# A RWKV-7 block solve: one transposed diagonal copied instead, two result copies regrouped on ScalarE, one value copy moved ahead

## The reference, cut to what matters

```python
def rwkv7_scan(r, w, kk, kka, k, v, s0):
    def step(S, inp):
        r_t, w_t, kk_t, kka_t, k_t, v_t = inp
        sa = jnp.einsum('bzhvk,bzhk->bzhv', S, -kk_t)
        S = S * w_t[..., None, :] + sa[..., None] * kka_t[..., None, :] + v_t[..., None] * k_t[..., None, :]
        return S, jnp.einsum('bzhvk,bzhk->bzhv', S, r_t)
```

## Time and profile before

| | |
|---|---|
| time, median of 3 runs | 3142.31 us (3141.88 to 3144.67) |
| the profiled execution: time, span | 3141.88 us, 3140.1 us |
| busy: PE / DVE / ACT / POOL | 96% / 58% / 34% / 13% |
| chain that ended last: PE / DVE / ACT | 83% / 8% / 3% |
| layer 0's chunks (843 to 1040 us): length, PE / DVE / POOL busy | 197.0, 169.0 / 137.6 / 64.9 us |
| layer 1's chunks (2383 to 2585 us): length, PE / DVE / POOL busy | 202.0, 172.8 / 134.3 / 65.0 us |

### The profile page before, as it was taken

The page is one execution under the profiler, slowest core; times in us unless marked ns, Lnnn a source line. Parts: engine busy times, 40 slices in busy tenths (PEclk is TensorE's granted clock), DMA queues, the critical chain, the costliest instruction groups (busy, mean ns, idle before and its releaser), DMA issues.

```text
span 3140.1 us, 62825 instructions
## 1 busy us (share of the span) xinstructions
PE 3005.7 (96%) x26760; PEld 2700.9 (86%) x26760; DVE 1823.1 (58%) x2658; ACT 1073.1 (34%) x1609; POOL 412.0 (13%) x465
## 2 busy tenths in 40 slices
PE   6999999999988899999999999999998889999998
PEld 5999978996777799998799998799776777999986
DVE  3767555656766767765657675633666666222235
ACT  3111244235443531113531113532454435211134
POOL 1000101002233310001100001110033323000100
PEclk9999999999899999999999999999998989999999
DMA  5344334310000333333433333422010003121134
GB/s 225 133 160 160 120 128 155 124 41 27 30 4 13 123 132 148 131 144 134 148 147 133 148 147 127 148 101 84 15 50 7 13 33 126 67 80 67 64 124 167
DMA packets 62635, 324.09 MB, mean 103 GB/s; under 512 B 8752, under 2 KB 12400, under 8 KB 42992
## 3 DMA queue, kind: packets, MB, share of 16 engines
q1 hardware_dynamic: 62448, 321.39, 27.9%
HBM read 318.05 MB, written 3.31 MB: 102 GB/s over the span
## 4 chain that ended last, share of the span: by engine, by line
PE 83%; DVE 8%; DMA 3%; issue 3%; ACT 3%; POOL 0%; SPq 0%; DVEq 0%; ACTq 0%; POOLq 0%
PE PS L2474 47%; PE PS L2557 16%; PE PS L2485 3%; DMA wo<-in_wo 3%; PE PS L696 2%; PE PS L1470 2%; DVE wo_lo L2876 1%; ACT wo_hi L2671 1%; PE PS L720 1%; PE PS L1449 1%; PE PS L643 1%; PE PS L1462 1%; DMA wm<-in_wm 1%; PE PS L708 1%; PE PS L1393 1%
## 5 line engine op out<-in xcount | busy, mean ns | idle before, releaser
L2474 PE MATMUL PS<-h_hi,wi_hi 128*128 128x384 f32 (+1 forms) x3360 | 799.0, 310 | 11.1 <-issue 10.9
L2474 PE MATMUL PS<-h_lo,wi_hi 128*128 128x384 f32 (+1 forms) x3360 | 797.3, 309 | 0.0
L2474 PE MATMUL PS<-h_hi,wi_lo 128*128 128x384 f32 (+1 forms) x3360 | 797.3, 309 | 0.0
L2474 PEld LDWEIGHTS PS<-h_hi,wi_hi 128*128 128x128 f32 x3360 | 526.3, 188 | 14.2 <-issue 13.4
L2474 PEld LDWEIGHTS PS<-h_hi,wi_lo 128*128 128x128 f32 x3360 | 526.2, 188 | 0.7
L2474 PEld LDWEIGHTS PS<-h_lo,wi_hi 128*128 128x128 f32 x3360 | 525.9, 188 | 0.7
L2557 PE MATMUL PS<-wo_hi,a_hi 128*128 128x512 f32 x968 | 392.9, 406 | 21.3 <-DVE wo_lo L2876 13.8
L2876 DVE TENSOR_TENSOR wo_lo<-wo,wo_hi 128x1024 fp32r<-128x1024 f32 x208 | 256.2, 1232 | 253.8 <-ACT wo_hi L2671 253.1
L2664 ACT ACTIVATE sg<-PS 128x640 f32<-128x640 f32 x88 | 62.2, 706 | 937.4 <-PE PS L2474 937.4
L2557 PE MATMUL PS<-wo_hi,a_lo 128*128 128x512 f32 x968 | 378.4, 391 | 0.0
L2557 PE MATMUL PS<-wo_lo,a_hi 128*128 128x512 f32 x968 | 378.1, 391 | 0.0
(11 more groups left out here) (324 smaller groups left out, 3804.2 us busy)
## 6 DMA issues: line engine op xcount, KB each, us to landing
wi<-in_wi SPq DMA_DIRECT2D x88, 1024.0 KB, 4.9
wo<-in_wo SPq DMA_DIRECT2D x176, 512.0 KB, 3.5
wm<-in_wm SPq DMA_DIRECT2D x36, 2048.0 KB, 7.4
wi<-in_win SPq DMA_DIRECT2D x24, 1024.0 KB, 5.2
wo<-in_wout SPq DMA_DIRECT2D x32, 512.0 KB, 3.5
wq<-in_wq SPq DMA_DIRECT2D x2, 1024.0 KB, 4.8
out_y_sample<-x SPq DMA_DIRECT2D x4, 512.0 KB, 5.5
lvl<-in_lvl SPq DMA_DIRECT2D x2, 896.0 KB, 6.0
```

Source lines behind the costliest of these rows:

```text
L2474: mm = pe.matmul(PSF[0:cols, at:at + GW[g]], st, h[g][:, k, :], start=(k == 0 and q == 0), stop=(k == KD - 1 and q == 2))
```

## The change

Three edits in `solve`, and the semaphores that they need. (1) On DVE the four transposes L2139 become four `tensor_copy` instructions from `XTc[1]`, the same size, SBUF to SBUF. (2) The copy of `Zs[1]` goes from DVE (L2157) to ACT, right behind `Zs[0]`; in the last chunk DVE's `beside(5)` therefore follows `beside(4)` directly, and ACT's `Zs[1]` stands ahead of its own `beside(5)`. (3) In chunks 0 to 3 ACT's `values_out(c, 0)` goes ahead of `diagonal(c)`. The two semaphores `t10` and `t11` become one, on which the two directions' events alternate.

```diff
-        stage("t10", 30)
-        stage("t11", 30)
+        series("level_lx_out", 30, "t10", "t11")
...
+                if not last:
+                    values_out(c, 0)
                 diagonal(c)
                 if last:
                     beside(3)
                 else:
-                    values_out(c, 0)
                     values_out(c, 1)
...
-                until(a_, l, "t1_mm0", 5 * c + 5)
-                a_.activation(Zs[0][64:P, :, :].rearrange("p h t -> p (h t)"), PS[64:P, 4 ^ f, :], ACT.Copy)\
-                    .then_inc(S["t10"].sem, 1)
+                for d in range(2):
+                    until(a_, l, f"t1_mm{d}", 5 * c + 5)
+                    b = slice(64, P) if d == 0 else slice(0, 64)
+                    a_.activation(Zs[d][b, :, :].rearrange("p h t -> p (h t)"), PS[b, (4 + 2 * d) ^ f, :], ACT.Copy)\
+                        .then_inc(S[f"t1{d}"].sem, 1)
...
                 for q in range(4):
                     at = slice(q * QUAD, (q + 1) * QUAD)
-                    m = v_.transpose(XT[1][at, :, at], Xc[1][at, :, :])
+                    m = v_.tensor_copy(XT[1][at, :, at], XTc[1][at, :, :])
                 m.then_inc(S["xt1"].sem, 1)
...
                 if last:
                     beside(3)
                     beside(4)
+                    beside(5)
                 else:
                     prep(c + 1, 2)
                     prep(c + 1, 3)
-                mm_("t1_mm1", 5 * c + 5)
-                mm_("gh_mm1", c)
-                v_.tensor_copy(Zs[1][0:64, :, :].rearrange("p h t -> p (h t)"), PS[0:64, 6 ^ flip(c), :])\
-                    .then_inc(S["t11"].sem, 1)
-                if last:
-                    beside(5)
-                else:
                     prep(c + 1, 4)
```

## The result

| | before | after |
|---|---|---|
| time, median (range) | 3142.36 us, 4 runs (3141.88 to 3144.67) | 3163.36 us, 4 runs (3161.49 to 3168.25) |
| profiled execution: time, span | 3141.88, 3140.1 us | 3157.67, 3155.9 us |
| ratio, 95% interval | | 1.0063 (1.0049 to 1.0077) |

The change made the kernel slower by 21 us; I had forecast 3153.1 us, and 3159 as the upper end. The direction was right and the size about half. The profiled execution took 3157.67 us, 15.8 more than the profiled one of before and 5.7 less than after's median, so the trace shows a quicker execution than the median one.

What follows compares the result with a forecast made beforehand. In chunks 0 to 3 DVE from L2010 to L2024 was taken to set the end. Terms 11.0 + 1.3 + 0.1 - 1.2 = +11.2 us gave 3153.1 us, range 3144 to 3159 (forecast's own 3150 to 3158).

Steps and rivals of the forecast that it cites:

- Which unit is held, and by what: Chunks 0 to 3: DVE's SBUF-to-SBUF copies wait while a POOL mask runs; free, 0.23 us each; transposes never over 309 ns.
- One copy through at each gap: Between POOL's masks one DVE copy gets in per gap; in chunk 2, L2010 starts 1.84 us later.
- the six chunks that I counted: All four of layer 0, chunks 1 and 2 of layer 1, where L2010 starts 0.13 behind POOL's end: +1.84 us each.
- the term of the held copies: L2010 delayed behind POOL's masks: 6 x 1.84 = +11.0 us, and +1.3 us in layer 1's chunk 0.
- through early: Rival, 0.20: copies finish before the third mask, which is stretched; 3145.2 us, or 3146.8 with two copies per gap.
- not held: Rival, 0.15: copies with stepped destination avoid the shared way, under 0.3 us beside masks; only -1.2 stays, 3140.7 us.
- One sign of a wrong forecast: L1417 no longer waiting for DVE would mean ACT's order or Zs[1] has become the limit.
- ACT's edits at 0, and −1.2 in the last chunks: Value copy first and Zs[1] on ACT hide in chunks 0 to 3; last chunks gain 0.6 us per layer.
- the clock was a rival with 0.04: More PE idling drops a few stretches to the lower clock, some 1.5 us each, up to 3159; chance beyond 3159: 0.04.

Runs made afterwards that it cites:

- the run with five matmuls: Changed kernel plus five 256-column PE matmuls, output overwritten, in front of L1455 in chunks 0 to 3: ratio 1.0033 to the kernel before.
- both stalls: Changed kernel with transposes back, in chunks 0 to 3 repeated by eight more transposes: ratio 1.0065; by four more: 1.0016, to the kernel before.
- the first four kernels: Against the kernel before: transposes back in the changed kernel 0.9982, copies alone 1.0056, eight more transposes without copies 1.0065, changed kernel plus ten matmuls 1.0062.

## Why the prediction was half right

**Which unit is held, and by what: right.** Copies of 0.2 us take up to 1.34 beside the masks, the transposes never over 0.31, and without masks none takes over 0.224 (forecast 0.23 free). The Trainium skill ("SBUF — State Buffer", section "Who interferes with whom") says of a VectorE copy in a two-port mode and a GpSimd instruction that whichever issues first has the shared port pair for the whole instruction and the other fully blocks; the trace agrees: two copies of chunk 2 last 1.21 us, as long as the masks' steps, and the masks stay at 1.25 to 1.29 us each.

**One copy through at each gap: right.** DVE's copies and POOL's last two masks in after's chunk 2, one by one:

```profile
952.63 1.02 DVE L2141 COPY XT<-XTc 32x128 f32<-32x128 f32 x1
953.66 1.21 DVE L2141 COPY XT<-XTc 32x128 f32<-32x128 f32 x1
954.89 1.21 DVE L2141 COPY XT<-XTc 32x128 f32<-32x128 f32 x1
956.11 0.22 DVE L2141 COPY XT<-XTc 32x128 f32<-32x128 f32 x1
...
953.53 1.27 POOL L2267 TENSOR_TENSOR LK<-LK,mask 128x512 f32<-128x512 f32 x1
954.75 1.27 POOL L2267 TENSOR_TENSOR LK<-LK,mask 128x512 f32<-128x512 f32 x1
```

The copies end at 953.65, 954.87, 956.10 and 956.33, the masks at 953.57, 954.80 and 956.02. The tiny copy falls to 0.17, L1455's delay grows by 2.40 (forecast 2.4), and L2012 starts 1.82 us later than L2010 had (4.44 to 6.26 behind L1677; forecast 1.84). In the six chunks that I counted it is 1.73 to 1.87, 10.9 together (forecast 11.0), and in layer 1's chunk 0 1.69 (forecast 1.3). So the term of the held copies, as DVE shows it, had the right size.

**The rivals "through early" and "not held": out.** The first asked for stretched masks and copies done before the third one, the second for copies under 0.3 beside a mask. Neither is there. One sign of a wrong forecast did come: L1416 no longer waits for DVE in seven chunks. I had written that this would make ACT's order or `Zs[1]` the limit. It is not so: with ACT's edits and no copies the loss is gone (0.9982), and what fills the wait is L1455 and its neighbours at the lower clock.

**ACT's edits at 0, and −1.2 in the last chunks: right in place.** Timeline of after, layer 0, chunk 4:

```profile
1044.48 1.97 PE L1710 MATMUL PS<-X,LB 64*64 64x128 f32 x16
...
1050.44 0.34 PE L1569 MATMUL PS<-X,btok 128*64 128x64 f32 x4 [0.88 <-DVE X L2164]
```

L1569 starts 5.96 us behind L1710; L1570 had started 6.56 behind L1711 (1029.62 to 1036.18, the latter in the earlier trace rows): 0.60 less, as forecast. In layer 1 it is 5.96 against 6.77.

**The step that failed: "held copies, 6 × 1.84 = +11.0 us" was made at PE's unchanged clock, and the clock was a rival with 0.04.** I wrote of it that "if a few stretches fell to the lower level, each might cost some 1.5 us". That price was near, though no row stood beside it; the count was not. L1455 ran at the lower level in seven of eight chunks, in six of them behind the stall. Chunk 2 of layer 0 splits cleanly: 8.88 us from L1678 to L1723 in before; 10.65 with the stall and the clock held up by filler, 1.77 more; 12.29 in after, 1.64 on top. The same split in the ratios: without copies 0.9982, with the copies and the filler 1.0033, with the copies 1.0063. So of 0.0081 for the copies, 0.0030, some 9 us, came back when five matmuls held the clock up; the other 0.0051, some 16 us, holds the stall and the filler's own lateness in three chunks. The runs of the three ratios were not made side by side, so the split of the total is rougher than that of the chunk.

The stall's own part can also be over my 1.84 a chunk. In two chunks of the run with five matmuls in which the clock was 1.00 from L1677 to the next chunk's, the next chunk starts 2.4 us later than in before (32.93 against 30.54 in layer 0's chunk 1, 32.98 against 30.55 in layer 1's chunk 0). In before these two had a wait of 0.29 before L1417 and L1723 at 8.25, where the chunks like chunk 2 had 0.51 and 8.88; their share of the delay was less covered, and in that run L2012 came 2.3 to 2.4 later.

**What the trace of before had to say on it.** I averaged: PE 84% busy in 12 us, 73% after, and found no row for a fall. But before's own last chunk had one. PE's timeline there, and its windows:

```profile
1012.90 1.11 PE L1510 MATMUL PS<-STa,RGs 64*128 64x64 f32 x16
...
1018.36 1.84 PE L1510 MATMUL PS<-STa,RGs 64*128 64x64 f32 x16 [1.71 <-ACT gate L981]
```

```profile
1008.00:1018.00 10.00, 7.89 (x226) 6.40 (x224) 7.47 (x20) 3.90 (x12) 1.86 (x2) 0.81 0.01 3
1018.00:1022.42 4.42, 4.06 (x24) 3.68 (x25) 4.16 (x11) 0.98 (x3) 0.00 (x0) 0.56 0.00 0
1022.42:1025.80 3.38, 3.36 (x17) 3.17 (x16) 3.25 (x7) 0.60 (x1) 1.84 (x2) 0.56 0.00 0
```

The same 16 matmuls take 1.11 us and then 1.84 behind an idle stretch of 1.71, and the clock is 0.56 for the next 7 us; from 1012.90 to 1018.36 it had been 1.00. With 2.4 us of new idle time in each of six chunks, this row says to count a slow stretch in each: 6 × 1.6 = 9.6 more, 3162.7 us, 0.7 from the median that was measured. That it lands so close is in part luck: the traced execution took 3157.67. That the fall follows the stall was only shown by the runs with stalls and fillers.

## What to carry to other kernels

A stall of PE has two prices: its own length less its cover, and the slow stretch behind it; look in the trace for idle stretches of the same length that are already there and read what like matmuls take behind them. Before an SBUF copy is put on DVE in place of another form, look at what POOL runs beside it; the same copy was 0.22 or 1.34 us. A conflict between two engines can be settled by moving the other side: masks that nobody waits for soon were moved by one wait, and the kernel with copies went from 1.0063 to 0.9973.

## What the runs showed of the hardware

- How long PE idled ahead of this product, with the clock at 1.00 up to there, and what followed, over the traces of after, copies alone, both stalls, before and the kernels without a stall: 1.96 to 2.75 us, lower clock behind it in 17 of 17; 1.86 us, once, clock kept; 1.39 to 1.46 us, lower in 2 of 4; 0.26 or 0.48 us, kept in 50 of 50. In the kernels without a stall 14 of 64 chunks still had the lower clock, each time already ahead of the product; what brought it there is open.
- The time of an execution goes with its mean granted clock, for the kernel before as well: of the 13 executions beside the first four kernels, 3138.4 us came with 0.980 and 3158.0 us with 0.973. So a part of the scatter is likely the number of such slow stretches (not shown by a trace of each).
- Where the whole stretch was at the lower level, 16 matmuls of 128 x 128 with their loads take 3.78 us instead of 2.05, and a transpose by PE 0.42 instead of 0.27.
- Where POOL products follow each other, exactly one waiting DVE copy got through at the end of each (in chunk 2 in both gaps between the last three masks), and POOL's next product was not lengthened by it (1.27 us).
- Matmuls whose result nobody reads held the granted clock at 1.00, but paid only where they fitted the gap: ten in a gap for five gave back nothing (1.0062 against 1.0063).
